# Reordering the preparation of a chunked recurrence on the GpSimd engine, together with the joins at the ends of the recurrence and of the kernel

## The reference, cut to what matters

```
def step(S, inp):
    r_t, w_t, k_t, v_t, kk_t, a_t = inp
    sa = jnp.einsum('bhij,bhj->bhi', S, -kk_t)
    S = (S * w_t[:, :, None, :]
         + sa[..., None] * (kk_t * a_t)[:, :, None, :]
         + v_t[..., None] * k_t[:, :, None, :])
```

## Time and profile before

| | |
|---|---|
| median of 3 runs | 2282.9 us (2282.88 to 2283.89) |
| profiled execution, its own time | 2284.2 us |
| its span in the profile | 2282.3 us |
| PE busy | 2251.7 us, 99% |
| DVE, ACT, POOL busy | 1244.3, 1014.6, 1113.5 us |
| mean granted clock of TensorE | 0.996 of full |

### The profile page before, as it was taken

How to read it: one execution, slowest core, us unless ns; L and a number is a source line. 1 busy time by engine, 2 the same in 40 slices (tenths; PEclk the granted TensorE clock), 3 DMA queues, 4 the chain that set the end, 5 groups by cost and what they waited for, 6 DMA issues and landing times.

```text
span 2282.3 us, 38543 instructions
## 1 busy us (share of the span) xinstructions
PE 2251.7 (99%) x14781; PEld 1907.6 (84%) x14781; DVE 1244.3 (55%) x2170; ACT 1014.6 (44%) x1707; POOL 1113.5 (49%) x691
## 2 busy tenths in 40 slices
PE   8999999999999999999999999999999999999998
PEld 7898887889988988888777778888988878888987
DVE  6662246268757641568555467714626996731642
ACT  5332235468754332365644265423434445432432
POOL 5344345544545454444666254443545983443442
PEclk9999999999999999999999999999999999999999
DMA  4233233320022333232110112332332332232331
GB/s 170 74 111 112 72 122 111 120 73 1 6 97 84 102 120 101 92 130 72 60 38 32 48 49 90 105 108 66 123 106 76 98 105 83 93 111 74 111 111 55
DMA packets 56310, 200.63 MB, mean 88 GB/s; under 512 B 6368, under 2 KB 6624, under 8 KB 56160
## 3 DMA queue, kind: packets, MB, share of 16 engines
q1 hardware_dynamic: 54576, 195.82, 26.0%
q10 hardware_dynamic: 1584, 2.75, 0.4%
HBM read 196.45 MB, written 2.10 MB: 87 GB/s over the span
## 4 chain that ended last, share of the span: by engine, by line
PE 69%; DVE 2%; ACT 1%; POOL 1%; issue 0%; DVEq 0%; POOLq 0%; ACTq 0%
PE ps L259 13%; PE ps L260 13%; PE ps L261 13%; PE ps L534 8%; PE ps L533 8%; PE ps L535 8%; PE ps L1185 1%; PE ps L2598 1%; PE ps L1199 1%; PE ps L2574 0%; PE ps L2594 0%; PE ps L2543 0%; PE ps L2645 0%; PE ps L2510 0%; ACT sb_later_p L1247 0%
## 5 line engine op out<-in xcount | busy, mean ns | idle before, releaser
L240 POOL TENSOR_TENSOR sb_w_lo<-sb_w_raw,sb_w_hi 128x1024 fp32r<-128x1024 f32 (+1 forms) x211 | 508.4, 2416 | 422.2 <-ACT sb_w_hi L227 381.5
L524 POOL TENSOR_TENSOR sb_w_lo<-sb_w_raw,sb_w_hi 128x1024 fp32r<-128x1024 f32 x122 | 297.7, 2451 | 270.6 <-ACT sb_w_hi L516 207.9
L227 ACT ACTIVATE sb_w_hi<-sb_w_raw 128x1024 fp32r<-128x1024 f32 x210 | 220.2, 1056 | 336.8 <-PE ps L261 309.6
L533 PE MATMUL ps<-sb_xn_hi,sb_w_hi 128*128 128x512 f32 (+1 forms) x1040 | 369.3, 355 | 0.0
L534 PE MATMUL ps<-sb_xn_lo,sb_w_hi 128*128 128x512 f32 (+1 forms) x1040 | 369.2, 355 | 0.0
L535 PE MATMUL ps<-sb_xn_hi,sb_w_lo 128*128 128x512 f32 (+1 forms) x1040 | 369.0, 355 | 0.0
L260 PE MATMUL ps<-sb_hid_lo,sb_w_hi 128*128 128x512 f32 x864 | 336.2, 389 | 0.0
L259 PE MATMUL ps<-sb_hid_hi,sb_w_hi 128*128 128x512 f32 x864 | 336.2, 389 | 0.0
L261 PE MATMUL ps<-sb_hid_hi,sb_w_lo 128*128 128x512 f32 x864 | 336.1, 389 | 0.0
L259 PE MATMUL ps<-sb_xn_hi,sb_w_hi 128*128 128x512 f32 (+1 forms) x536 | 220.2, 411 | 1.5 <-DVEq L309 1.5
L533 PEld LDWEIGHTS ps<-sb_xn_hi,sb_w_hi 128*128 128x128 f32 x1040 | 196.6, 189 | 28.7 <-DVE sb_rs L459 0.4
(11 more groups left out here) (536 smaller groups left out, 4412.7 us busy)
## 6 DMA issues: line engine op xcount, KB each, us to landing
sb_w_raw<-weights SPq DMA_DIRECT2D x365, 512.0 KB, 3.4
sb_stage<-x SPq DMA_DIRECT2D x4, 512.0 KB, 5.0
out<-sb_out_stage SPq DMA_DIRECT2D x8, 256.0 KB, 2.9
sb_abias<-table ACTq DMA_DIRECT2D x4, 256.0 KB, 4.4
sb_lora_w<-lora ACTq DMA_DIRECT2D x2, 256.0 KB, 2.8
sb_rstd<-table ACTq DMA_DIRECT2D x1, 256.0 KB, 2.6
sb_root<-table ACTq DMA_DIRECT2D x1, 256.0 KB, 4.9
sb_ss<-table ACTq DMA_DIRECT2D x1, 256.0 KB, 4.9
```

What stands on the lines that cost most here:

```text
L227: act.activation(c.w_hi[:, slot, 0:width], c.w_raw[:, slot, 0:width], ACT.Copy).then_inc(c.s_hi, 1)
L240: pool.tensor_tensor(c.w_lo[:, slot, 0:width], c.w_raw[:, slot, 0:width], c.w_hi[:, slot, 0:width].bitcast(F32), ALU.subtract).then_inc(c. ...
L524: pool.tensor_tensor(c.lo_blocks[:, both].rearrange("p b k n -> p (b k) n"), c.w_raw[:, x.u % RING], c.hi_blocks[:, both].rearrange("p b k ...
L533: pe.matmul(out, hi, rhs_hi(k), start=start and k == 0, stop=False)
```

## The change

There are five edits.

1. POOL's order in the preparation of every pair: b0, B, K and A are made before `le` instead of after it. B now waits for ePi, A for ePn, and Bp for ePe; before, A waited for ePe.
2. In pair 0, PE waits for A instead of K, and DVE makes `raw2` of pair 1 after the first masks (before the `lab` mask) instead of before `prod`'s masks.
3. At the start of attention in the recurrence's end, ACT makes the two copies of k's low part (L2876) before the tail's root and `softmax(0)`; DVE makes `scale(0)` after `yn` and two halves of a query's low part; POOL waits for two negated maxima before the weight subtraction of unit base + 22.
4. At the kernel's end the last square goes to SBUF and is not added by DVE: PE sums the first seven tiles' squares and the last square in one accumulation. The table for the root is loaded one tile earlier, by a root of a constant.
5. The turned tiles of the second half use two other PSUM banks, so that they don't wait for the first half's outputs.

```
 def layer_end_act(...)
+        if n == KD - 1 and last_square is not None:
+            act.activation(c.root_t[:, 0:1], c.eps[:], ACT.Sqrt)
...
-        act.activation(c.ps[:, 4 + n % 2], new, ACT.Square).then_inc(c.s_sq, 1)
+        square = c.ps[:, 4 + n % 2] if n < KD - 1 or last_square is None else last_square
+        act.activation(square, new, ACT.Square).then_inc(c.s_sq, 1)
 def layer_end_dve(...)
-        else:
+        elif n < KD - 1 or last_square is None:
             dve.wait_ge(c.s_ss, KD * i + n)
             dve.tensor_tensor(c.ss[:], c.ps[:, 4 + n % 2], c.ss[:], ALU.add).then_inc(c.s_ss, 1)
 def rwkv_pe(...)
         if j == 0:
-            PL(j, "K")
+            PL(j, "A")
 def rwkv_act(...)
-    tail(PAIRS - 1, "yroot")
-    softmax(0)
     for side in range(2):
         act.wait_ge(m.s_klo, side + 1)
         act.activation(m.k_lo[HALF[1 - side], 2 + side], ...)
+    tail(PAIRS - 1, "yroot")
+    softmax(0)
     softmax(1)
 def rwkv_pool(...)
         prepared("lp", pool.tensor_tensor(w.ePp, w.L[:], w.ld[:], ALU.subtract))
-        lw = chunks(w.L[:])
-        prepared("le", pool.tensor_tensor(chunks(w.ePe), ..., lw, ALU.subtract))
         if j >= 1:
             stream_low(pool, c, base + 8 + 3 * j, base + 9 + 3 * j)
         PV(j, "kk")
-        PA(j, "ePe")
-        prepared("A", pool.tensor_tensor(w.AR[:, 0], w.kk[:], w.ePp, ALU.mult))
         prepared("b0", pool.tensor_tensor(w.tmp, w.kk[:], w.a[:], ALU.mult))
+        PA(j, "ePi")
         mine(j, "b0")
         prepared("B", pool.tensor_tensor(w.BK[:, :, 0], chunks(w.tmp), chunks(w.ePi), ALU.mult))
         prepared("K", pool.tensor_tensor(w.BK[:, :, 1], chunks(w.k[:]), chunks(w.ePi), ALU.mult))
+        PA(j, "ePn")
+        prepared("A", pool.tensor_tensor(w.AR[:, 0], w.kk[:], w.ePp, ALU.mult))
+        lw = chunks(w.L[:])
+        prepared("le", pool.tensor_tensor(chunks(w.ePe), ..., lw, ALU.subtract))
+        PA(j, "ePe")
         prepared("Bp", pool.tensor_tensor(w.BKp[:, 0], w.tmp, w.ePe, ALU.mult))
...
     attention_prepare(3)
+    pool.wait_ge(a.s_negmax, 2)
     stream_low(pool, c, base + 22, base + 23)
 def rwkv_dve(...)
-        prepare(q, "raw")
+        prepare(q, "raw10" if j == 0 else "raw")
         E(j, "prod")
...
+        if j == 0:
+            prepare(q, "raw2")
         E(j, "lab")
...
     maxima(1)
-    scale(0)
     tail(t, "yn")
     query_low(1, 0, 10)
     query_low(1, 1, 10)
+    scale(0)
 def output_pe(...)
-    for t in range(TT):
-        turn(0, t)
-    pe.wait_ge(c.s_ss, KD * (i + 1))
+    turn(0, 0)
+    turn(0, 1)
+    pe.wait_ge(c.s_ss, KD * (i + 1) - 1)
+    (four products of c.ss with ones, start at t == 0, stop=False)
+    turn(0, 2)
+    pe.wait_ge(c.s_sq, KD * i)
     (four products, now of c.sq[:, 0] with ones, start=False, stop=True)
     mm.then_inc(c.s_msum, 1)
+    turn(0, 3)
```

More of the change, by code:

```diff
@@ L974, in layer_end_act @@
 def layer_end_act(act, c, base, nk, i, gain=None, gain_sq=None, kept=None, ahead=None,
-                  banks=None):
+                  banks=None, last_square=None):
     per = -(-nk // KU)
@@ L1014, in layer_end_dve @@
 def layer_end_dve(dve, c, base, nk, i, coef, scaled_base=None, gain=None, gain_sq=None, bias=None,
-                  finished=None, banks=None):
+                  finished=None, banks=None, last_square=None):
     per = -(-nk // KU)
@@ L2156, in rwkv_preparation @@
     dve = ["raw1", "raw0", "raw2", "kmax", "rec", "L", "kk", "bon"]
-    pool = ["k", "kk0", "r", "v", "ka", "kfin", "rk", "lp", "le", "A", "b0", "B", "K", "Bp", "Kp", "pend", "R"]
+    pool = ["k", "kk0", "r", "v", "ka", "kfin", "rk", "lp", "b0", "B", "K", "A", "le", "Bp", "Kp", "pend", "R"]
     return pe, act, dve, pool
@@ L2937, in rwkv_pool @@
         prepared("lp", pool.tensor_tensor(w.ePp, w.L[:], w.ld[:], ALU.subtract))
-        lw = chunks(w.L[:])
-        prepared("le", pool.tensor_tensor(chunks(w.ePe), lw[:, :, CH - 1:CH].broadcast_to([P, NCH, CH]), lw, ALU.subtract))
         if j >= 1:
@@ L2948, in rwkv_pool @@
         prepared("K", pool.tensor_tensor(w.BK[:, :, 1], chunks(w.k[:]), chunks(w.ePi), ALU.mult))
+        PA(j, "ePn")
+        prepared("A", pool.tensor_tensor(w.AR[:, 0], w.kk[:], w.ePp, ALU.mult))
+        lw = chunks(w.L[:])
+        prepared("le", pool.tensor_tensor(chunks(w.ePe), lw[:, :, CH - 1:CH].broadcast_to([P, NCH, CH]), lw, ALU.subtract))
+        PA(j, "ePe")
         prepared("Bp", pool.tensor_tensor(w.BKp[:, 0], w.tmp, w.ePe, ALU.mult))
@@ L3071, in prepare @@
         b_w, b_norm, b_turned = preparation_banks(base + 2 + 3 * j, j)
-        if part == "raw":
+        if part in ("raw", "raw10", "raw2"):
             for x, last in ((1, "A"), (0, "K"), (2, "Kp")):
+                if x == 2 and part == "raw10" or x < 2 and part == "raw2":
+                    continue
                 if j >= 1:
@@ L3078, in prepare @@
                 prepared(f"raw{x}", dve.tensor_tensor(w.raw[:, x, 1:], ps[:, unit % RING], c.rs[:], ALU.mult))
+            if part == "raw10":
+                return
             mine(j, "raw2")
@@ L3769, in output_bank @@
     free = ((base + 1) % RING, (base + 3) % RING, 6, 7)
-    return free[t] if h == 0 or t >= 2 else ((base + 2 * (KD - 2)) % RING, 5)[t]
+    return free[t] if h == 0 else ((base + 2 * (KD - 2)) % RING, 5, (base + 2 * (KD - 1)) % RING, SUM_BANK)[t]
 def output_act(act, c, i, base):
@@ L3804, in turn @@
         mm.then_inc(c.s_tout, 1)
+    turn(0, 0)
+    turn(0, 1)
+    pe.wait_ge(c.s_ss, KD * (i + 1) - 1)
     for t in range(TT):
-        turn(0, t)
-    pe.wait_ge(c.s_ss, KD * (i + 1))
+        pe.matmul(c.ps[:, SUM_BANK, t:t + 1], c.ss[:, t * P:t * P + P], c.ones[:, 0:1], start=t == 0, stop=False,
+                  skip_group_check=True)
+    turn(0, 2)
+    pe.wait_ge(c.s_sq, KD * i)
     for t in range(TT):
-        mm = pe.matmul(c.ps[:, SUM_BANK, t:t + 1], c.ss[:, t * P:t * P + P], c.ones[:, 0:1], start=True, stop=True)
+        mm = pe.matmul(c.ps[:, SUM_BANK, t:t + 1], c.sq[:, 0, t * P:t * P + P], c.ones[:, 0:1], start=False, stop=True,
+                       skip_group_check=True)
     mm.then_inc(c.s_msum, 1)
+    turn(0, 3)
     for t in range(TT):
@@ L3815, in output_pe @@
         elif t == 2:
-            pe.wait_ge(c.s_out_dve, LOADED + 2)
+            pe.wait_ge(c.s_evac, base + 2 * KD + START)
         elif t == 3:
-            pe.wait_ge(c.s_out_act, LOADED + 2)
+            pe.wait_ge(c.s_root, ROOTS[i])
         turn(1, t)
@@ L4053, in mlp @@
                 up(name + "_upB", F1A, False, f + F1A, i)
-                layer_end_act(act, c, B[name + "_downB"], F1A, i + 1, following, kept=kept)
+                layer_end_act(act, c, B[name + "_downB"], F1A, i + 1, following, kept=kept,
+                              last_square=c.sq[:, 0] if following is None else None)
             ffn("ffn1", 0, 0, gain("mix_norm"))
@@ L4135, in mlp @@
                 up(name + "_upB", F1A, False, f + F1A, i)
-                layer_end_dve(dve, c, B[name + "_downB"], F1A, i + 1, 1.0, scaled + KD, following)
+                layer_end_dve(dve, c, B[name + "_downB"], F1A, i + 1, 1.0, scaled + KD, following,
+                              last_square=c.sq[:, 0] if following is None else None)
             input_dve(dve, c)
```

## The result

The changed kernel takes 2296.55 us (median of 6 runs, 2295.09 to 2297.2), the kernel before 2282.89 (6 runs, 2281.89 to 2285.15): the ratio is 1.0058, with an interval of 1.0047 to 1.0069. It is slower by 13.7 us; forecast were +13.2. Its profiled execution took 2295.09, with a span of 2293.1; that of before took 2284.2, with a span of 2282.3.

The account below looks back on a forecast made before the run. PE was taken as the bound everywhere, busy 2251.7 of 2282.3 us. The terms +14.8 + 5.1 - 1.3 - 4.8 - 0.6 = +13.2 us, added to 2282.9, gave 2296.1 us; range 2289 to 2302.

Parts of the forecast that it names:

- stalls at `ru`: Pairs 1 to 3: PE waits at `ru` for ACT's u copy, queued behind ePe, which waits for POOL's later `le`; +14.8 us.
- clock behind them: After the three waits at `ru`, PE's clock drops, costing 1.7 us each, +5.1 us in all (0 to 8.4).
- pair 0: Edits 1 and 2 in pair 0: PE's waits before `prod` and `lab` go, ACT's turned copies then limit; -1.3 us.
- attention: Edit 3, start of attention: gate product's wait shrinks by 2.45 us and the clock stays up; -4.8 us.
- end: Edits 4 and 5, kernel's end: PE's last sum starts 0.6 us sooner, outputs stay paced by DMAs; -0.6 us.
- Rival A: ACT's u copy can go ahead of ePe, so edit 1 costs nothing: -6.7 us, 2276.2 us, faster; 6%.
- D: Part of the stall at `ru` is hidden: half of 14.8 us and no clock loss, +0.7, 2283.6 us; 5%.
- C: After each stall at `ru` the clock stays down to the pair's end: up to 29 us in all, 2320 us; 4%.
- rival B: Attention gains 2.4 instead of 4.8 us, as the shorter wait drops the clock or diagonals come late: 2298.5 us; 10%.
- good terms: The gains forecast for pair 0, attention and the end: -1.3, -4.8 and -0.6, together -6.7 us.

## Why the prediction was right, step by step

| term | forecast | profile | by times |
|---|---|---|---|
| stalls at `ru` | +14.8 (5.3, 4.85, 4.6) | +14.9 (5.26, 4.80, 4.83) | |
| clock behind them | +5.1 (0 to 8.4) | +3.9 (1.2, 1.8, 0.9) | +5.3 and +3.6 |
| pair 0 | -1.3 (1.05 to 2.3) | -1.35 at `prod`, -1.1 at `ru` | -1.6 |
| attention | -4.8 (2.45 to 5.9) | -4.99 | -2.3 (parts -2.2, -3.5) |
| end | -0.6 (0 to 0.8) | -0.75 | -1.4 |
| sum | +13.2 | | +13.7 |

*The stall* held in each of its parts. POOL reached b0, B, K and A at the steps forecast, ACT waited 6.6 us for `le`, and pairs 1 and 2 are within 0.05. Pair 3 came 0.2 longer: the kernel before, from which it was read, has 4.49 us there from the start of `le` to `ru`, where the kernels with the attention edit alone and the end alone have 4.26 and 4.28, as in pair 2. That the way from `le` to `ru` is a queue was shown by moving ePe, not argued from the order of rows. Rival A is refuted, and D with it: nothing hides a part of the stall.

*The clock behind the stalls* was near in sum, and there luck had a part. Each period from `prod` to `prod` can be cut at `ru`, and the wait taken off. Of the 4.17 us by which the three periods grew beyond their waits (19.06 - 14.89), only 3.93 stand behind a stall: 1.18, 1.84 and 0.91 us more from `ru` to the next `prod`. The lower clock lasted 5.9, 4.4 and 3.5 us beyond the start of `ru` there. Two other drops cancel: the changed kernel has one at 1184 to 1190 with no wait in front of it, which costs 1.18, and the kernel before had one at 1228 to 1232, which cost it 1.18 as well; the remaining 0.24 are what pair 0 loses again between `prod` and `ru`. The term was built from that row of 1228 to 1232, priced at 1.7. It was worth 1.2: from `prod` to `ru` are 30.86 us with the drop and 29.60 to 29.69 in the kernels without it. So the price of the row was too high, the drops behind the stalls lasted longer than the row's, and the two errors partly made up for each other. C is refuted: the clock came back within 6 us of `ru` each time.

*Pair 0*: both waits left, and ACT's turned copies became the limit, as forecast: `lv` moved 0.72 us ahead where the pair began 0.43 later, 1.15 in all. K's turn got a wait of 0.8 us that wasn't forecast, for the mask of `lab`, in front of which `raw2` now stands on DVE; as ACT was the limit, it seems to have cost nothing more. POOL's A ended at 1115.93, not near 1115.1, because b0 took 2.27 us beside a DVE subtraction of 128x1024 (2.31 us); PE came at 1116.42 and lost nothing by it.

*Attention* is the term that was mis-sized. The waits were right: 2.45 forecast, 2.43 shown; 0.65 us left, 0.84 shown. The step that doesn't hold is the price of the clock: it took the loss of the one profiled execution, 2.4 us, for what the edit saves in the median. That execution had one of the two longest drops of the six seen in that place, and lay 1.3 us above its median. With their mean the edit is worth 4.0; the medians of the runs say 2.3, with an interval from 0.5 to 4.8. That holds 4.0 and just reaches the forecast, so how much of it is missing stays open. 2.3 is near rival B's 2.4, but B's means are refuted: neither did the shorter wait drop the clock, nor were the diagonals late (their POOL row ends at 1345.44, and PE goes from the scores to the turn at 1345.46 without a gap). The prediction also said that the moved subtraction could hold `scale(0)` until its end. It didn't: the reciprocal took 0.18 us in the midst of it (1343.93, with the subtraction from 1341.91 to 1344.29).

*The end* gave 0.75, by the chain that was named; behind the first scaled output both kernels take 8.0 us, at the DMAs' pace.

The forecast of the sum of the good terms, -6.7, was met by the two kernels that have them without the stall, -6.6 and -6.7, both faster than either kernel of this case. How it splits over the three terms isn't shown by the times. The single edits' medians add up to -5.3; the difference of 1.3 is no more than the single intervals leave (each about 2 us to either side). The ledger's -1.59 in pair 3 need not be owed to the change. From `prod` to `ru` the kernel before has 37.41 us there and the changed kernel 35.83, but the kernel with the end's edits alone, whose recurrence is that of before, has 35.83 too, and the twelve profiled executions spread between the two. What remains open: what makes that spread (before had an idle time of 1.3 us near 1282), and the clock between 1184 and 1190 in the changed kernel, where no wait of PE stands in front.

## What to carry to other kernels

When a step is moved to a later place on one engine, follow its reader to the engine it sits on and ask what is queued behind the reader: here PE needed nothing made from `le` for another 15 us (1152.27 to 1167.39 in the kernel with ePe moved), but the copy of u stood behind its exponential, and each us beyond a slack of 1.65 to 2.1 became a us of stall. The cure can be to move the reader and not the step; here it gave the same 2276 us as undoing the move. And a loss of clock read from one profiled execution is no price: the same place cost 0 to 2.5 us by the execution. Nor is it half of the time at the lower clock: 5.9 us of it cost 1.2, 3.6 us cost 0.1.

## What the runs showed of the hardware

The lower clock behind an idle time of PE isn't fixed by the kernel. The same wait of 3.09 us, before the same product, was followed in six executions once by nothing, three times by 3 to 4 us and twice by 5.6 us or more at 1.2 GHz. Three waits of 2.7 to 3.2 us were followed by nothing in the one execution of that kernel whose trace was kept; the four others took 4 to 7 us longer. Of three waits up to 1.9 us one was followed by a drop. Drops also came without a wait of over 1 us in front: at 1228 to 1232 (two executions), at 1184 to 1190 (one), and at 507 to 511 or 514, far ahead of every edit, in six of the twelve profiled executions, which reach the first `prod` 1.3 to 3.2 us later than others with the same preparation of pair 0. That is a part of the spread from which the single edits could not be told.

The Trainium skill, TensorE: Matmul & The Clock Gate, section What's actually happening, says of the slow matmuls at a kernel's start that their number varies between runs of one kernel, with the phase that the activity monitor has when the kernel starts. The drops here are in the midst of the kernel; they vary too, but no trace shows the monitor's phase, so whether it is for that reason isn't shown.

A small DVE instruction (the negated maximum, 128x4) takes 2.16 to 2.18 us when it starts beside a POOL subtraction of 128x1024, and ends as that ends; without, it takes 0.17. Not every small one is held: the reciprocal of 128x4 took 0.18 beside the same subtraction. A POOL product of 128x512 takes 2.27 instead of 1.29 beside a DVE subtraction of 128x1024. The held maximum cost the path a third of a us here.
